# Down projection with weight panels of 512 rows by 512 columns in place of 1024 by 256, and one matmul bank a token tile held over two panels

## The chip, the cores and the metric

One core of one Trainium2 chip. The metric is the device time of one execution in microseconds (us). A core has TensorE (PE) for matmuls, whose weight loads are shown apart as PEld, VectorE (DVE), ScalarE (ACT), GpSimd (POOL) and SyncE (SP); SP and POOL issue most of the transfers.

## The reference

One inference step of a decoder layer of width 1024, over 2048 prompt tokens and 32 sample tokens (8 requests of 4). The part that the change touches is the MLP:

```python
D_MODEL = 1024; SEQ = 2048; DEC_BATCH = 8; DEC_SEQ = 4; D_FF = 4 * D_MODEL
...
    o = jnp.concatenate([y_a, y_b, y_c, y_d], axis=-1) @ w_out
    x = x + rms_norm(o, g_mix_post)
    f = rms_norm(x, g_ffn_pre)
    f = jnp.square(jax.nn.relu(f @ w_up)) @ w_down
    x = x + rms_norm(f, g_ffn_post)
```

Ahead of it stand an input projection (1024 to 2048 columns) and four parallel mixers (pooling, a 31-tap convolution, a chunked gating, a short convolution), whose outputs are concatenated for w_out. All arrays are float32.

## The kernel before

**Precision.** A projection in float32 is made of three matmuls in the format fp32r. Each operand is split in two parts: "hi" is its value rounded to fp32r, "lo" the rest. The helper `three` (L1772) issues hi x hi, hi x lo and lo x hi into the same bank, for each of K = 8 slices k of 128 rows of the contraction.

**Blocks and stages.** The tokens are worked in NB = 4 blocks of N1 = 512; the last block also carries the 32 sample tokens. First the input projection and the mixers run for all blocks ("I" panels), then block by block the output projection ("O"), and the MLP in Q = 4 quarters q of the hidden width: an up stage "U" makes 1024 hidden columns, and a down stage "D" multiplies them with 1024 rows of w_down and adds to the result of the earlier quarters in SBUF. In the last quarter of a block the O panels and the transposes of the next block stand among the D panels. The list `order` holds all panels.

**Panels.** A panel is a weight piece of 1024 rows by PC = 256 columns, [128, 8, 256] in SBUF. A stage has NP = 4 of them. Two slots s = j % 2 alternate. SP loads panel j into `raw[s]`; ACT rounds it into `w_hi[s]` (`split_hi`, L677), once the panel j - 2, which used the slot, is done on TensorE (`wait_panel`); DVE writes `w_lo[s]` (`split_lo`, L1127); TensorE starts panel j when `lo_ready` says so.

**Which operand moves.** In a U panel the weight slice is the stationary operand (128 x 128) and the tokens move: 512 columns of `act_hi` or `act_lo` at a time, 256 or 288 in the last block. The result has hidden columns on the partitions. ACT takes relu out of the bank and squares it (`squared_relu`, L949 and L951), DVE makes `u_hi[:, k]` and `u_lo[:, k]` (`u_parts`, L1498 and L1500); k runs with the panels, two a panel. In a D panel 128 tokens of `u_hi` or `u_lo` are stationary and the weight panel moves, 256 columns at a time. The result has tokens on the partitions; the four token tiles of a block lie two to a bank (`token_banks`), and the 32 sample tokens have a bank of their own.

**Banks.** Six banks `mm0` to `mm5` go round in a ring (`bank_of`). TensorE waits with `take_bank` until a bank is free; `bank_done` tells of its last matmul, `bank_free` that it was read. A D panel of quarter 0 is copied out by ACT (`d_copy`, L966), of quarters 1 to 3 added by DVE (`d_add`, L1516), to `f2_sb` (the profile's name for it is f_sb). On ACT and DVE a panel's split for j + 2 stands just ahead of the panel's last bank (`token_panel`).

Of the kernel before, what the change touches and what calls it, by code (L numbers as in the profile page):

```python
# [5 lines left out]
def hybrid_trunk_step(nc, x_prompt, x_sample, state_pool, state_conv, state_short, g_mix_pre, g_mix_post,  # L6
# [9 lines left out]
    PE, DVE, SC, GP = nc.tensor, nc.vector, nc.scalar, nc.gpsimd  # L16
# [53 lines left out]
    def token_banks(b):  # L70

        pairs = [[(2 * i + h, (2 * i + h) * P, P) for h in range(2)] for i in range(NCH // 2)]
        return pairs if b < NB - 1 else pairs + [[(NCH, N1, NS)]]

    NRING = 6
# [1 line left out]
    bank_of, wrote, freed, turn = {}, [0] * NRING, [0] * NRING, 0  # L79
    for j in range(J2, NPAN):  # L80
        kind, b, q, p = order[j]
        n_banks = 2 * len(halves(b)) if kind == "U" else len(token_banks(b))
        for i in range(n_banks):
            bank = turn % 4 if j < J2 + NP else (turn - 2 * NP + 4) % NRING
            turn += 1
            wrote[bank] += 1
            bank_of[j, i] = (bank, wrote[bank], freed[bank])
            freed[bank] += 1
        bank_of[j, "last"] = bank_of[j, n_banks - 1]
# [10 lines left out]
    with ctx:  # L100
# [261 lines left out]
        y_ready = sem("y_ready")  # L362
        y_out = sem("y_out")
        y_last = sem("y_last")

        OUT_SMALL = 2 + 3 * NB_S + 1 + 3
        WIN = [(0, 0, 2), (HEAD, 0, 4), (0, 1, 8), (HEAD, 1, 16)]
# [13 lines left out]
        def source(j):  # L381
            kind, b, q, p = order[j]
            if kind == "I":
                return w_in_v[:, :, COLS[p]:COLS[p] + PC]
            if kind == "O":
                return w_out_v[:, :, p * PC:(p + 1) * PC]
            if kind == "U":
                return w_up_v[:, :, q * D + p * PC:q * D + (p + 1) * PC]
            return w_dn_v[q][:, :, p * PC:(p + 1) * PC]

        def wait_panel(eng, j):

            if j < 0:
                return
            if j < NI:
                eng.wait_ge(zs_done, j + 1)
            elif j < J2:
                eng.wait_ge(tile_done, 2 * (j + 1))
            else:
                bank, done, _ = bank_of[j, "last"]  # L400
                eng.wait_ge(bank_done[bank], done)
# [59 lines left out]
        def _(sp):  # L461
# [16 lines left out]
            for j, (kind, b, q, p) in enumerate(order):  # L478
                s = j % 2
                if j not in part_no:  # L480
                    if j in (J2, J2 + 1):
                        sp.wait_ge(x_tr, 2 * NCH * NB)
                    elif s in raw_user:
                        sp.wait_ge(lo_ready, split_no[raw_user[s]])
                    if j >= 2:
                        sp.dma_start(raw[:, s, :, :], source(j)).then_inc(raw_full[s], 16)
                    raw_user[s] = j
                if j == 3:
                    sp.wait_ge(bias_ready, 1)
# [178 lines left out]
        def _(act):  # L668
# [284 lines left out]
            def d_copy(j, i):  # L953
                _, b, q, p = order[j]
                bank = bank_of[j, i][0]
                tiles = token_banks(b)[i]
                tile, n, nt = tiles[0][0], tiles[0][2], len(tiles)
                wait_bank(act, j, i)
                if b > 0:
                    act.wait_ge(y_out, 16 * NCH * b)  # L960
                elif p == 0:
                    act.wait_ge(sx_tr, 1)
                    act.wait_ge(out_small, 16 * OUT_SMALL)
                    if i == 1:
                        act.wait_ge(smp_st, 64)
                SC.activation(f2_sb[0:n, tile:tile + nt, p * PC:(p + 1) * PC],  # L966
                              mm[bank][0:n, 0:nt * PC].rearrange("p (h c) -> p h c", h=nt), ACT.Copy)\
                  .then_inc(bank_free[bank], 1)

            def y_squares(j, i):  # L970
                _, b, q, p = order[j]
# [21 lines left out]

            def token_panel(j, piece):
                _, b, q, p = order[j]
                n = len(token_banks(b))
                for i in range(n):
                    if i == n - 1:
                        split_hi(j + 2)
                    piece(j, i)  # L1000
# [118 lines left out]
        def _(dve):  # L1119
# [383 lines left out]
            def d_add(j, i):  # L1503
                _, b, q, p = order[j]
                bank = bank_of[j, i][0]
                tiles = token_banks(b)[i]
                tile, n, nt = tiles[0][0], tiles[0][2], len(tiles)
                f2 = f2_sb[0:n, tile:tile + nt, p * PC:(p + 1) * PC]
                if q == 1:
                    before = index("D", b, 0, p)  # L1510
                else:
                    before = index("D", b, q - 1, p)
                old, _, free = bank_of[before, i]
                dve.wait_ge(bank_free[old], free + 1)
                wait_bank(dve, j, i)
                DVE.tensor_tensor(f2, mm[bank][0:n, 0:nt * PC].rearrange("p (h c) -> p h c", h=nt), f2, ALU.add)\  # L1516
                   .then_inc(bank_free[bank], 1)

            def y_inverse(b, g=0):
# [31 lines left out]

            def token_panel(j, piece):
                _, b, q, p = order[j]
                n = len(token_banks(b))
                for i in range(n):
                    if i == n - 1:
                        split_lo(j + 2)
                    piece(j, i)
# [212 lines left out]
        def _(pe):  # L1771
# [272 lines left out]
            for j in range(J2, NPAN):  # L2044
# [16 lines left out]
                            i += 1  # L2061
                else:
                    hi, lo = (act_hi, act_lo) if kind == "O" else (u_hi, u_lo)
                    for i, bank_tiles in enumerate(token_banks(b)):
                        bank = take_bank(j, i)
                        for h, (tile, t0, n) in enumerate(bank_tiles):
                            for k in range(K):
                                if kind == "O" and p == 0 and k == 0:
                                    pe.wait_ge(mix_lo, no(b, tile) + 1)
                                if kind == "D" and p == 0 and i == 0 and h == 0:  # L2070
                                    pe.wait_ge(u_lo_ready, u_no(b, q, k, len(halves(b))))
                                last_mm = three(mm[bank][0:n, h * PC:(h + 1) * PC], hi[:, k, t0:t0 + n],
                                                lo[:, k, t0:t0 + n], w_hi[:, s, k, :], w_lo[:, s, k, :], k)
                            if h == len(bank_tiles) - 1:
                                last_mm.then_inc(bank_done[bank], 1)
                            if kind == "D" and q == Q - 1 and b < NB - 1:
# [58 lines left out]
```

## Time and profile before

| | |
|---|---|
| median of 3 runs | 2232.03 us (2230.04 to 2232.41) |
| the profiled execution's own time | 2230.47 us |
| its span | 2228.2 us |
| mean granted TensorE clock over the span | 0.983 |
| PE busy | 2122.0 us, 95% of the span |
| PEld busy (beside PE) | 1932.4 us, 87% |
| DVE, ACT, POOL busy | 1083.2, 754.6, 107.6 us |
| DMA traffic | 287.42 MB |

The profiled execution's own time is 2.27 us more than its span and 1.56 us less than the median of the runs. Sums below are made from durations of this one execution, and are set against its own time. A matmul's duration in the profile overlaps the next one's, since matmuls are pipelined; what one costs in a stream is the distance between two starts.

### The profile page before, as it was taken

To read this page: it belongs to the slowest core of one execution; us is meant where nothing else is said; L and a number is where in the kernel's file an instruction comes from. 1 tells how busy PE (TensorE), PEld (TensorE's weight loads), DVE (VectorE), ACT (ScalarE), POOL (GpSimd) and SP (SyncE) were. 2 spreads that over 40 slices of the span, in tenths; PEclk is the share of its full clock that TensorE was granted. 3 is DMA by queue.
4 is the path that set the end of the run, shared out by engine and by line. 5 is a ranking of instruction groups with operands and counts; after the bars stand their busy time and mean duration, and the time that the engine had idled before them with its cause. 6 is when DMAs were issued, how large, how long until landed. Compare 5 with 4: busy or idle time off the path is not lost.

```text
span 2228.2 us, 33002 instructions
## 1 busy us (share of the span) xinstructions
PE 2122.0 (95%) x14425; PEld 1932.4 (87%) x14425; DVE 1083.2 (49%) x1404; ACT 754.6 (34%) x1159; POOL 107.6 (5%) x190
## 2 busy tenths in 40 slices
PE   6999999994999999999999999999999989999997
PEld 5887778784798898989899898889899989999997
DVE  3687786866523334563333346533334553333334
ACT  4424232234233223443322344332324432314132
POOL 2011111110000000000000000000000000000000
PEclk9999999997899999999999999999999999999999
DMA  7754646553132223444233344533334333222231
GB/s 250 277 201 165 222 170 209 194 178 129 59 114 95 95 95 114 139 150 153 94 107 95 97 132 152 170 95 95 95 95 135 108 103 116 77 93 78 77 95 41
DMA packets 184836, 287.42 MB, mean 129 GB/s; under 512 B 5967, under 2 KB 162292, under 8 KB 176484
## 3 DMA queue, kind: packets, MB, share of 16 engines
q1 hardware_dynamic: 160868, 169.99, 23.9%
q0 software_dynamic: 22784, 114.28, 14.6%
q8 instruction: 114, 1.87, 0.3%
q10 hardware_dynamic: 1040, 1.05, 0.1%
q14 instruction: 30, 0.25, 0.0%
HBM read 245.01 MB, written 40.57 MB: 128 GB/s over the span
## 4 chain that ended last, share of the span: by engine, by line
PE 83%; DVE 7%; ACT 4%; DMA 3%; issue 2%; POOL 0%; ACTq 0%; POOLq 0%; DVEq 0%
PE mm L1773 27%; PE mm L1775 27%; PE mm L1774 27%; ACT w_hi L677 2%; DVE w_lo L1127 2%; DMA mixc<-mixT_scratch 1%; DVE conv L1171 1%; PE tr L1778 1%; DMA x_in<-in_x_prompt 1%; DMA raw<-in_w_in 1%; PE tr L2002 1%; ACT junk_y L976 0%; PE mm L1833 0%; PE tr L1799 0%; DVE f_sb L1516 0%
## 5 line engine op out<-in xcount | busy, mean ns | idle before, releaser
L1127 DVE TENSOR_TENSOR w_lo<-raw,w_hi 128x2048 fp32r<-128x2048 f32 x152 | 348.4, 2292 | 696.4 <-ACT w_hi L677 696.4
L1773 PE MATMUL mm<-act_hi,w_hi 128*128 128x512 f32 (+2 forms) x1728 | 632.2, 366 | 11.1 <-DVE act_lo L1484 5.8
L1775 PE MATMUL mm<-act_hi,w_lo 128*128 128x512 f32 (+2 forms) x1728 | 632.3, 366 | 0.0
L1774 PE MATMUL mm<-act_lo,w_hi 128*128 128x512 f32 (+2 forms) x1728 | 625.9, 362 | 0.0
L1773 PE MATMUL mm<-w_hi,u_hi 128*128 128x256 f32 (+1 forms) x2176 | 603.2, 277 | 1.7 <-DVE u_lo L1500 0.9
L1774 PE MATMUL mm<-w_lo,u_hi 128*128 128x256 f32 (+1 forms) x2176 | 600.8, 276 | 0.0
L1775 PE MATMUL mm<-w_hi,u_lo 128*128 128x256 f32 (+1 forms) x2176 | 600.8, 276 | 0.0
L677 ACT ACTIVATE w_hi<-raw 128x2048 fp32r<-128x2048 f32 x152 | 290.8, 1913 | 579.1 <-PE mm L1775 572.9
L1773 PEld LDWEIGHTS mm<-w_hi,u_hi 128*128 128x128 f32 (+1 forms) x2176 | 398.2, 183 | 4.9 <-DVE u_lo L1500 3.8
L1774 PEld LDWEIGHTS mm<-w_lo,u_hi 128*128 128x128 f32 (+1 forms) x2176 | 398.3, 183 | 1.1
L1775 PEld LDWEIGHTS mm<-w_hi,u_lo 128*128 128x128 f32 (+1 forms) x2176 | 398.2, 183 | 0.7
L1773 PEld LDWEIGHTS mm<-act_hi,w_hi 128*128 128x128 f32 x1728 | 328.3, 190 | 62.9 <-issue 14.9
L1774 PEld LDWEIGHTS mm<-act_lo,w_hi 128*128 128x128 f32 x1728 | 328.2, 190 | 57.1 <-issue 2.4
L1775 PEld LDWEIGHTS mm<-act_hi,w_lo 128*128 128x128 f32 x1728 | 327.5, 190 | 50.5
L1773 PE MATMUL mm<-w_hi,act_hi 128*128 128x256 f32 (+1 forms) x736 | 205.9, 280 | 7.0 <-DVE act_lo L1432 4.3
L1774 PE MATMUL mm<-w_lo,act_hi 128*128 128x256 f32 (+1 forms) x736 | 203.9, 277 | 0.0
L1775 PE MATMUL mm<-w_hi,act_lo 128*128 128x256 f32 (+1 forms) x736 | 203.9, 277 | 0.0
L949 ACT ACTIVATE square<-mm 128x512 f32<-128x512 f32 (+2 forms) x160 | 81.8, 511 | 257.7 <-PE mm L1775 255.1
L1171 DVE SCALAR_TENSOR_TENSOR conv<-g_ext,cst,conv 128x512 f32<-128x512 f32 x240 | 163.0, 744 | 0.7 <-ACT conv L800 0.7
L1498 DVE CAST u_hi<-square 128x512 fp32r<-128x512 f32 (+2 forms) x160 | 60.0, 375 | 187.6 <-ACT square L951 187.6
L1773 PEld LDWEIGHTS mm<-w_hi,act_hi 128*128 128x128 f32 (+1 forms) x736 | 131.2, 178 | 9.4 <-issue 5.1
L1774 PEld LDWEIGHTS mm<-w_lo,act_hi 128*128 128x128 f32 (+1 forms) x736 | 131.2, 178 | 2.0 <-issue 0.5
(244 smaller groups left out, 1341.7 us busy)
## 6 DMA issues: line engine op xcount, KB each, us to landing
raw<-in_w_ffn_up SPq DMA_DIRECT2D x64, 1024.0 KB, 5.4
raw<-in_w_ffn_down SPq DMA_DIRECT2D x64, 1024.0 KB, 5.2
w_hi<-whi_scratch POOLq DMA_DIRECT2D x24, 1024.0 KB, 5.2
w_lo<-wlo_scratch POOLq DMA_DIRECT2D x24, 1024.0 KB, 7.9
raw<-in_w_out SPq DMA_DIRECT2D x16, 1024.0 KB, 5.2
whi_scratch<-w_hi POOLq DMA_DIRECT2D x8, 1024.0 KB, 8.6
wlo_scratch<-w_lo POOLq DMA_DIRECT2D x8, 1024.0 KB, 10.8
mixc<-mixT_scratch POOLq DMA_DIRECT2D x16, 512.0 KB, 5.8
```

What stands on the lines that cost most here:

```text
L677: SC.activation(w_hi[:, s, :, :], raw[:, s, :, :], ACT.Copy).then_inc(hi_ready, 1)
L949: SC.activation(square[:, at % 2, 0:c1 - c0], mm[bank][:, 0:c1 - c0], ACT.Relu).then_inc(bank_free[bank], 1)
L1127: DVE.tensor_tensor(w_lo[:, s, :, :], raw[:, s, :, :], w_hi[:, s, :, :].bitcast(fp32), ALU.subtract)\
L1171: DVE.scalar_tensor_tensor(out=c, in0=g_ext[:, t, k:k + N1], scalar=col("conv_w", 2 * k + t), in1=c, op0=ALU.mult, op1=ALU.add).then_inc(c ...
L1498: DVE.tensor_copy(u_hi[:, k, c0:c1], square[:, at % 2, 0:c1 - c0]).then_inc(u_hi_ready, 1)
L1773: PE.matmul(out, whi, xhi, start=(k == 0), stop=False)
L1774: PE.matmul(out, whi, xlo, start=False, stop=False)
L1775: return PE.matmul(out, wlo, xhi, start=False, stop=(k == K - 1))
L1778: PE.matmul(bank[:, 0:n], headmean[:, :], src, start=True, stop=True).then_inc(done, 1)
L2002: last = PE.transpose(tr[hh][:, kk * P:kk * P + n], f_sb[0:n, m % 2, k * P:(k + 1) * P], ident[0:n, 0:n])
```

## The change

For the quarters q = 0, 1, 2 of each block (12 of the 16 down stages; `wide(j)` says which) the four panels of a stage keep their number and their size of 1 MB, but have another form. Panels 0 and 1 hold output columns 0 to 511, panels 2 and 3 columns 512 to 1023; the even one holds rows k = 0 to 3 of the contraction, the odd one k = 4 to 7. The slots are the same memory, seen as [128, 4, 512]. Each token tile takes a bank of its own (four, or five in the last block) in the even panel, and its accumulation is finished in the odd one. The moving operand is 512 weight columns. Since no bank is done in an even panel, a new semaphore `half_done` tells when its last matmul is through; ACT and DVE have only their split in an even panel, and read all banks out in the odd one.

```diff
+    def wide(j):
+        return order[j][0] == "D" and order[j][2] < Q - 1
+
+    def panel_banks(j):
+        banks = token_banks(order[j][1])
+        return [[t] for bank in banks for t in bank] if wide(j) else banks
...
-        n_banks = 2 * len(halves(b)) if kind == "U" else len(token_banks(b))
+        n_banks = 2 * len(halves(b)) if kind == "U" else len(panel_banks(j))
+        if wide(j) and p % 2:
+            for i in range(n_banks):
+                bank_of[j, i] = bank_of[j - 1, i]
+            bank_of[j, "last"] = bank_of[j, n_banks - 1]
+            continue
...
+            if wide(j):
+                return w_dn_v[q][:, p % 2 * (K // 2):(p % 2 + 1) * (K // 2), p // 2 * 2 * PC:(p // 2 + 1) * 2 * PC]
...
+            elif j in half_no:
+                eng.wait_ge(half_done, half_no[j])
...
             def d_copy(j, i):
...
-                elif p == 0:
+                elif p == 1:
...
-                SC.activation(f2_sb[0:n, tile:tile + nt, p * PC:(p + 1) * PC],
-                              mm[bank][0:n, 0:nt * PC].rearrange("p (h c) -> p h c", h=nt), ACT.Copy)\
-                  .then_inc(bank_free[bank], 1)
+                c = p // 2 * 2 * PC
+                SC.activation(f2_sb[0:n, tile, c:c + 2 * PC], mm[bank][0:n, :], ACT.Copy).then_inc(bank_free[bank], 1)
...
+                if j in half_no:
+                    split_lo(j + 2)
+                    return
...
+                    if wide(j):
+                        w_h, w_l = (as_panel(w[:, s, :, :], j) for w in (w_hi, w_lo))
+                        for i, ((tile, t0, n),) in enumerate(panel_banks(j)):
+                            bank = bank_of[j, i][0] if p % 2 else take_bank(j, i)
+                            for kk in range(K // 2):
+                                k = p % 2 * (K // 2) + kk
+                                if p < 2 and i == 0:
+                                    pe.wait_ge(u_lo_ready, u_no(b, q, k, len(halves(b))))
+                                last_mm = three(mm[bank][0:n, :], hi[:, k, t0:t0 + n], lo[:, k, t0:t0 + n],
+                                                w_h[:, kk, :], w_l[:, kk, :], k)
+                            if p % 2:
+                                last_mm.then_inc(bank_done[bank], 1)
+                        if p % 2 == 0:
+                            last_mm.then_inc(half_done, 1)
+                        continue
```

On TensorE the first tile of a down stage looks like this before; each group of three belongs to one slice k, and the eight that wait for `u_lo_ready` are k = 0 to 7 (block 0, quarter 1; shown are k = 0, the head of k = 1, and k = 7):

```order
L1773 MATMUL mm<-w_hi,u_hi 128x256 [waits u_lo_ready,bank_free4,lo_ready]
L1774 MATMUL mm<-w_lo,u_hi 128x256
L1775 MATMUL mm<-w_hi,u_lo 128x256
L1773 MATMUL mm<-w_hi,u_hi 128x256 [waits u_lo_ready]
...
L1773 MATMUL mm<-w_hi,u_hi 128x256 [waits u_lo_ready]
L1774 MATMUL mm<-w_lo,u_hi 128x256
L1775 MATMUL mm<-w_hi,u_lo 128x256
```

and like this in the changed kernel, where the lines of `three` are 1810 to 1812. The tile has four slices and goes over to the next bank:

```order
L1810 MATMUL mm<-w_hi,u_hi 128x512 [waits u_lo_ready,bank_free4,lo_ready]
L1811 MATMUL mm<-w_lo,u_hi 128x512
L1812 MATMUL mm<-w_hi,u_lo 128x512
L1810 MATMUL mm<-w_hi,u_hi 128x512 [waits u_lo_ready]
...
L1810 MATMUL mm<-w_hi,u_hi 128x512 [waits bank_free5]
L1811 MATMUL mm<-w_lo,u_hi 128x512
```

So the waits for k = 4 to 7 now stand at the head of panel 1, behind the four tiles of panel 0. A stage of 384 matmuls of 256 columns (480 in the last block, with the sample tile) becomes one of 192 (240) of 512 columns.

On ACT the four panels of block 0, quarter 0 read before (a copy takes a bank with two tiles of 256 columns, and the split stands between the two copies of a panel):

```order
L966 ACTIVATE f_sb<-mm 128x2x256 [waits out_small,sx_tr,bank_done0]
L677 ACTIVATE w_hi<-raw 128x2048 [waits bank_done1,raw_full0]
L966 ACTIVATE f_sb<-mm 128x2x256 [waits out_small,smp_st,sx_tr,bank_done1]
L966 ACTIVATE f_sb<-mm 128x2x256 [waits bank_done2]
L677 ACTIVATE w_hi<-raw 128x2048 [waits bank_done3,raw_full1]
L966 ACTIVATE f_sb<-mm 128x2x256 [waits bank_done3]
```

for panels 0 and 1, and in the changed kernel for the same two:

```order
L709 ACTIVATE w_hi<-raw 128x2048 [waits half_done,raw_full0]
L998 ACTIVATE f_sb<-mm 128x512 [waits out_small,sx_tr,bank_done0]
L998 ACTIVATE f_sb<-mm 128x512 [waits out_small,smp_st,sx_tr,bank_done1]
L998 ACTIVATE f_sb<-mm 128x512 [waits out_small,sx_tr,bank_done2]
L709 ACTIVATE w_hi<-raw 128x2048 [waits bank_done3,raw_full1]
L998 ACTIVATE f_sb<-mm 128x512 [waits out_small,sx_tr,bank_done3]
```

The number of copies and their size stay; none stands in the even panel, and three stand ahead of the split in the odd one.

## Rows read from the trace of the kernel before

**Rows 1.** The page: busy times and the chain that ended last

```profile
PE 2122.0 (95%) x14425; PEld 1932.4 (87%) x14425; DVE 1083.2 (49%) x1404; ACT 754.6 (34%) x1159; POOL 107.6 (5%) x190
...
PE 83%; DVE 7%; ACT 4%; DMA 3%; issue 2%; POOL 0%; ACTq 0%; POOLq 0%; DVEq 0%
PE mm L1773 27%; PE mm L1775 27%; PE mm L1774 27%; ACT w_hi L677 2%; DVE w_lo L1127 2%; DMA mixc<-mixT_scratch 1%; DVE conv L1171 1%; PE tr L1778 1%; DMA x_in<-in_x_prompt 1%; DMA raw<-in_w_in 1%; PE tr L2002 1%; ACT junk_y L976 0%; PE mm L1833 0%; PE tr L1799 0%; DVE f_sb L1516 0%
```

**Rows 2.** Windows, the twelve down stages: stretch, length, PE busy (matmuls), clock, DMA

```profile
613.64:657.30 43.66, 43.66 (x386) 1.00 0.40 122
701.46:745.44 43.98, 43.83 (x386) 1.00 0.30 96
...
1018.08:1062.04 43.96, 43.81 (x386) 1.00 0.43 132
...
1853.51:1907.94 54.43, 54.43 (x482) 1.00 0.27 88
...
sum 558.72, PE 557.52; mean PE 46.46
```

**Rows 3.** The same view, up stages of block 1, 512 token columns moving

```profile
1062.04:1106.19 44.15, 44.15 (x194) 1.00 0.30 96
```

**Rows 4.** Timeline of PE, block 3: up of 256 and 288 columns, then down

```profile
1847.54 0.28 PE L1773 MATMUL mm<-act_hi,w_hi 128*128 128x256 f32 x1
...
1850.34 0.29 PE L1773 MATMUL mm<-act_hi,w_hi 128*128 128x288 f32 x1
...
1853.51 0.28 PE L1773 MATMUL mm<-w_hi,u_hi 128*128 128x256 f32 x1
```

**Rows 5.** Timeline of PE in block 0 at a low clock, 512 columns moving

```profile
561.62 0.63 PE L1775 MATMUL mm<-act_hi,w_lo 128*128 128x512 f32 x1
562.05 0.63 PE L1773 MATMUL mm<-act_hi,w_hi 128*128 128x512 f32 x1
```

**Rows 6.** Windows, the stretch around rows 5: length, PE busy, clock, DMA

```profile
561.19:565.03 3.84, 3.84 (x10) 0.50 0.00 0
```

**Rows 7.** Timeline of PE, first tile of the down stage at 1018.08

```profile
1018.08 0.28 PE L1773 MATMUL mm<-w_hi,u_hi 128*128 128x256 f32 x1
...
1020.36 0.28 PE L1775 MATMUL mm<-w_hi,u_lo 128*128 128x256 f32 x1
1020.79 0.38 PE L1773 MATMUL mm<-w_hi,u_hi 128*128 128x256 f32 x1
1021.01 0.28 PE L1774 MATMUL mm<-w_lo,u_hi 128*128 128x256 f32 x1
```

**Rows 8.** Timeline of ACT, same stage

```profile
1018.28 0.60 ACT L949 ACTIVATE square<-mm 128x512 f32<-128x512 f32 x1 [4.25 <-PE mm L1775]
1018.91 0.63 ACT L951 ACTIVATE square<-square 128x512 f32<-128x512 f32 x1
...
1030.23 0.60 ACT L966 ACTIVATE f_sb<-mm 128x512 f32<-128x512 f32 x1 [8.88 <-DMA out<-f_sb]
1030.72 1.91 ACT L677 ACTIVATE w_hi<-raw 128x2048 fp32r<-128x2048 f32 x1
```

**Rows 9.** Timeline of DVE, same stage

```profile
1019.58 0.43 DVE L1498 CAST u_hi<-square 128x512 fp32r<-128x512 f32 x1 [3.44 <-ACT square L951]
1020.04 0.69 DVE L1500 TENSOR_TENSOR u_lo<-square,u_hi 128x512 fp32r<-128x512 f32 x1
...
1032.67 2.29 DVE L1127 TENSOR_TENSOR w_lo<-raw,w_hi 128x2048 fp32r<-128x2048 f32 x1 [6.54 <-ACT w_hi L677]
```

**Rows 10.** Lines with shapes apart: reads of the banks in down stages

```profile
L1516 DVE TENSOR_TENSOR f_sb<-mm,f_sb 128x512 f32<-128x512 f32 x96 | 65.9, 687 | 80.3 <-PE mm L1775 80.3
L966 ACT ACTIVATE f_sb<-mm 128x512 f32<-128x512 f32 x32 | 18.8, 591 | 75.4 <-PE mm L1775 48.7 <-DMA out<-f_sb 26.7
```

**Rows 11.** The page: transfers of weights, KB each, us to landing

```profile
raw<-in_w_ffn_up SPq DMA_DIRECT2D x64, 1024.0 KB, 5.4
raw<-in_w_ffn_down SPq DMA_DIRECT2D x64, 1024.0 KB, 5.2
```

More of the change, by code:

```diff
@@ L364, in hybrid_trunk_step @@
         y_last = sem("y_last")
+        half_done = sem("half_done")
         OUT_SMALL = 2 + 3 * NB_S + 1 + 3
@@ L388, in source, with as_panel @@
                 return w_up_v[:, :, q * D + p * PC:q * D + (p + 1) * PC]
+            if wide(j):
+                return w_dn_v[q][:, p % 2 * (K // 2):(p % 2 + 1) * (K // 2), p // 2 * 2 * PC:(p // 2 + 1) * 2 * PC]
             return w_dn_v[q][:, :, p * PC:(p + 1) * PC]
+        def as_panel(slot, j):
+            if wide(j):
+                return slot.rearrange("p k c -> p (k c)").rearrange("p (k c) -> p k c", k=K // 2)
+            return slot
+        half_no = {}
+        for j in range(NPAN):
+            if wide(j) and order[j][3] % 2 == 0:
+                half_no[j] = 1 + len(half_no)
         def wait_panel(eng, j):
@@ L485, in _ @@
                     if j >= 2:
-                        sp.dma_start(raw[:, s, :, :], source(j)).then_inc(raw_full[s], 16)
+                        sp.dma_start(as_panel(raw[:, s, :, :], j), source(j)).then_inc(raw_full[s], 16)
                     raw_user[s] = j
@@ L955, in d_copy @@
                 bank = bank_of[j, i][0]
-                tiles = token_banks(b)[i]
-                tile, n, nt = tiles[0][0], tiles[0][2], len(tiles)
+                tile, _, n = panel_banks(j)[i][0]
                 wait_bank(act, j, i)
@@ L995, in token_panel @@
                 _, b, q, p = order[j]
-                n = len(token_banks(b))
+                n = len(panel_banks(j))
+                if j in half_no:
+                    split_hi(j + 2)
+                    return
                 for i in range(n):
@@ L1505, in d_add @@
                 bank = bank_of[j, i][0]
-                tiles = token_banks(b)[i]
+                tiles = panel_banks(j)[i]
                 tile, n, nt = tiles[0][0], tiles[0][2], len(tiles)
-                f2 = f2_sb[0:n, tile:tile + nt, p * PC:(p + 1) * PC]
-                if q == 1:
-                    before = index("D", b, 0, p)
-                else:
-                    before = index("D", b, q - 1, p)
-                old, _, free = bank_of[before, i]
-                dve.wait_ge(bank_free[old], free + 1)
+                if wide(j):
+                    f2 = f2_sb[0:n, tile:tile + 1, p // 2 * 2 * PC:(p // 2 + 1) * 2 * PC]
+                else:
+                    f2 = f2_sb[0:n, tile:tile + nt, p * PC:(p + 1) * PC]
+                for t, _, _ in tiles:
+                    old, _, free = bank_of[index("D", b, q - 1, p // 2 * 2), t]
+                    dve.wait_ge(bank_free[old], free + 1)
                 wait_bank(dve, j, i)
-                DVE.tensor_tensor(f2, mm[bank][0:n, 0:nt * PC].rearrange("p (h c) -> p h c", h=nt), f2, ALU.add)\
+                DVE.tensor_tensor(f2, mm[bank][0:n, 0:2 * PC if wide(j) else nt * PC].rearrange("p (h c) -> p h c", h=nt), f2, ALU.add)\
                    .then_inc(bank_free[bank], 1)
@@ L1553, in token_panel @@
                 _, b, q, p = order[j]
-                n = len(token_banks(b))
+                n = len(panel_banks(j))
+                if j in half_no:
+                    split_lo(j + 2)
+                    return
                 for i in range(n):
@@ L2063, in _ @@
                     hi, lo = (act_hi, act_lo) if kind == "O" else (u_hi, u_lo)
+                    if wide(j):
+                        w_h, w_l = (as_panel(w[:, s, :, :], j) for w in (w_hi, w_lo))
[12 more added lines that the diff above has]
+                        continue
                     for i, bank_tiles in enumerate(token_banks(b)):
```

## Prediction

> **What bounds the kernel now.** I read the page first. PE is busy for 2122.0 of 2228.2 us, and the chain that ended last lies on it for 83%, 27% on each of the three lines of `three` [rows 1]. DVE and ACT are busy for half the time or less. So only two things can move the time: what a matmul costs in a full stream, and the few places where the stream stops.
>
> The windows over the twelve down stages that the change touches show both [rows 2]. Each stage of blocks 0 to 2 has 384 matmuls of 256 columns (the counts in the windows are one or two higher, since they take in the neighbours at the edges), each of block 3 has 480. They take 558.72 us together. The stages of block 3 take 54.43 us, or 113.4 ns a matmul. At that distance 384 take 43.55 us. The first stage takes 43.66; the other eight of blocks 0 to 2 take some 43.97 (two of them are shown), so about 0.42 us is lost in each of the eight.
>
> The timeline shows where. In the stage that begins at 1018.08, the first 20 matmuls come at 114 ns, then the one at 1020.36 is followed only at 1020.79, 0.43 us on, and that by one after 0.22 us [rows 7]; a usual pair would take 0.23 of these 0.65 us. The late matmul is number 22, the first of slice k = 7. It waits for `u_lo_ready`: relu at 1018.28, square at 1018.91, u_hi at 1019.58, and u_lo from 1020.04 to 1020.73 [rows 8, 9]. That chain begins when the last up matmul has ended, and the seven slices ahead of k = 7 cover only some 2.4 us of it.
>
> **The change part by part.**
>
> *The wait for the last hidden slices.* In the changed program the first tile of a stage uses only k = 0 to 3; k = 7 comes first in panel 1, behind 48 matmuls of 512 columns, some 10.9 us on. u_lo of k = 7 is ready 2.65 us into the stage [rows 7, 9], and that of k = 3 was made two up panels ago. The hole goes, in eight stages: 8 x 0.42 = 3.4 us less. Nothing else is late next: the weights of panel 0 were there already when the stream went in without a gap.
>
> *The distance of the matmuls.* 4896 of 256 columns (9 x 384 + 3 x 480) become 2448 of 512 columns. The trace has no matmul that streams 512 weight columns past a token tile. The rows bound it from both sides. From above: in the up stages 192 matmuls of 512 token columns take 44.15 us, 229.9 ns each, more than two of the 256 weight columns (226.8) [rows 2, 3]. From below: if what a matmul takes beyond one column per cycle is a fixed price for each. That price: at a granted clock of 1.2 GHz 512 columns take 0.43 us [rows 5, 6], which is one column a cycle; at 2.4 GHz 256 columns are then 106.7 ns, and the row says 113.4. If the 6.7 ns are paid once a matmul, 512 columns take 220.0 ns.
>
> I take 226.8, twice the old distance, because the rows of the up stages speak for a price by the column. In block 3 the same kind of matmul, token columns moving, comes with 256 and with 288 columns: 24 of 256 from 1847.54 to 1850.34 are 116.7 ns each, 24 of 288 from 1850.34 to 1853.51 are 132.1 [rows 4]; with 512 it is 229.9. From 256 to 512 columns the distance rises by 113.2 ns, not by 106.7, and from 256 to 288 by 15.4, not by 13.3. A fixed price would not rise at all. What is left over, 3.3 ns a matmul, separates the two forms at equal length (116.7 against 113.4), and hangs on which operand moves, or where it lies in memory, rather than on how many columns there are. The moving operand here is the weight tile, as before. So the sum for this part is nil, with -16.6 us at one end (2448 x 6.8) and +7.6 us at the other (2448 x 3.1).
>
> The Trainium skill ("TensorE: Matmul & The Clock Gate", section "Back-to-back issue gap") gives the gap of two warm matmuls as the columns over 2.4 GHz plus some 2.5 ns. That is a fixed price; by it each merged pair would save 2.5 ns, 6.1 us in all. The trace does not agree with its figures: it has 113.4 where the rule gives 109.2, and 229.9 where it gives 215.8 [rows 2, 3].
>
> *Weights.* A panel stays 1 MB, and 48 matmuls of twice the length take as long as 96. The source rows are 2 KB in place of 1 KB. A load lands in 5.2 us [rows 11], and it has more than a panel of 10.9 us for it, so a change in its speed is hidden. The split of the next panel but one takes 1.91 us on ACT and 2.29 us on DVE; in the stage shown it ends at 1034.96 [rows 8, 9], and panel 2 begins at some 1040.3 (1018.08 + 0.42 + 192 x 0.1134), so 5.3 us are left. There the split had even stood behind a copy that waited 8.88 us for an output transfer [rows 8]; in the even panels of the changed kernel no copy stands ahead of it. In the odd ones three reads do, 0.59 us on ACT and 0.69 us on DVE [rows 10], and each of their banks is full 2.7 us before the next, so they are done when the split can begin. Price: nil; without that cover a late split would stop TensorE for its whole delay.
>
> *Banks and reads.* A bank is now held for over a panel. A stage takes four of the six in each pair of panels (five in block 3), in turn. The next pair begins with the free one or two, and its second or third tile, 2.7 us or more on, takes a bank that was full three quarters of a panel earlier. The last bank of a pair is read behind a split, 4.3 us + 0.69 us after its last matmul, and is taken again two or more tiles into a later panel. Price: nil, cover 2.7 us or more. The reads keep their number and width.
>
> **Sum.** The profiled execution took 2230.47 us. Less 3.4 us it is 2227.1 us. The median of the runs is 1.56 us above that execution, so 2228.6 us, 0.15% less than before. A difference under 0.2% (4.5 us) is about what a measurement of this kernel cannot tell from no change.
>
> **The rivals.**
>
> *A fixed price for each matmul* (faster). The new distance is 220.0 ns: 2448 x 0.220 = 538.6 us in place of 558.7, so -20.1 us and 2211.9 us. For it: the trace has no row of this form, and one column a cycle holds at the low clock. Against it: the 113.2 ns that 256 more token columns cost. A third of the price would be 3.4 + 5.5 us less, 2223.1 us. Chance 0.10 for the full price, 0.05 for about a third of it. The rule of "TensorE: Matmul & The Clock Gate" in the Trainium skill is this rival with 2.5 ns as the price: 3.4 + 6.1 us less, 2222.5 us.
>
> *The up stages' distance* (slower). If the 3.1 ns that 512 token columns have over twice 113.4 come from the long stream itself, the down stages take 2448 x 0.2299 = 562.8 us, 4.1 us more than now though the holes are gone: 2236.1 us. It decides from 228.2 ns on, where the loss eats the 3.4 us. For it: it is the only row with 512 columns in this format at full clock. Against it: 256 token columns carry the same surplus. Chance 0.15; about half of that would measure over +0.2%.
>
> *The hole only moves.* If the first tile still stopped, at its head or at panel 1, for 0.42 us, nothing would change: 2232.0 us. It would need k = 3 or the weights of panel 0 to be late, and both were there. Chance 0.06.
>
> *The forecast* has the rest, 0.64: holes gone, twice the distance. Its own range is 2225 to 2231 us, and with the scatter of the runs (1 to 2 us) about a sixth of it falls beyond -0.2%.
>
> **How the numbers follow.** Faster by over 0.2%: 0.15 + 0.11 = 0.26. Slower by over 0.2%: 0.08. Within: 0.66. The range from 2221 to 2238 us takes in the forecast, the moved hole, the up stages' distance and a third of the fixed price, and leaves out the full fixed price and mishaps, not over 0.2.
>
> **What would show it.** In the profile after, the distance of two matmuls of 512 columns in a down stage: 226.8 (forecast), 220 (fixed price) or 230 (up stages' distance). A wide stage of blocks 0 to 2 should last 43.5 us, of block 3 54.4 us, with no gap at k = 7 in its first tile and none at the head of panel 1. The up stages should stay at 44.15 us, and the fourth quarters should keep their hole, which the change does not reach. The forecast is wrong if TensorE waits for ACT or DVE at a panel's head (a bank or a split late), or if the time moves outside the twelve stages.

## The result and the profile after

The changed kernel takes 2247.18 us (median of 4 runs, 2244.35 to 2247.47) against 2231.03 us (4 runs, the three from before and one more, 2229.93 to 2232.41): ratio 1.0069, interval 1.0052 to 1.0087, that is 12 to 19 us slower. The forecast was 2228.6 us, range 2221 to 2238. The profiled execution took 2247.47 us with a span of 2245.6 us (before 2230.47 and 2228.2).

The page of the changed kernel, against [rows 1, 11]: busy times, chain, and the loads of the down weights.

```profile
PE 2137.6 (95%) x11977; PEld 1831.2 (82%) x11977; DVE 1082.5 (48%) x1400; ACT 755.4 (34%) x1157; POOL 107.2 (5%) x190
...
PE 84%; DVE 7%; ACT 4%; DMA 3%; issue 2%; POOL 0%; ACTq 0%; POOLq 0%; DVEq 0%
...
raw<-in_w_ffn_down SPq DMA_DIRECT2D x64, 1024.0 KB, 5.0
```

There are 2448 matmuls fewer, and PE is busy 15.6 us longer. The windows over the same stages, against [rows 2] (stretch, length, PE busy with the matmuls, granted clock, DMA share, GB/s):

```profile
617.62:662.29 44.67, 44.67 (x195) 1.00 0.40 119
706.45:751.03 44.58, 44.58 (x193) 1.00 0.31 95
...
1026.07:1070.65 44.58, 44.58 (x193) 1.00 0.42 130
...
1867.14:1922.85 55.71, 55.71 (x242) 1.00 0.27 85
...
sum 568.44, PE 568.44; mean PE 47.37
```

Two things are read here. Length and busy time are equal in every stage, where before 43.96 stood beside 43.81: TensorE no longer stops. And still each stage is longer: 44.58 us over 192 matmuls is 232.2 ns each, 55.71 over 240 is 232.1. Together they take 568.44 us in place of 558.72, +9.7 us. It is the same at a DMA share of 0.31 and of 0.42, so it isn't the transfers. An up stage of block 1, against [rows 3], hasn't moved:

```profile
1070.65:1114.82 44.17, 44.17 (x194) 1.00 0.28 96
```

The timeline of PE shows the head of the down stage at 1026.07 and, 48 matmuls on, the head of its panel 1, the places of [rows 7]:

```profile
1025.84 0.39 PE L1812 MATMUL mm<-act_hi,w_lo 128*128 128x512 f32 x1
1026.07 0.39 PE L1810 MATMUL mm<-w_hi,u_hi 128*128 128x512 f32 x1
1026.30 0.39 PE L1811 MATMUL mm<-w_lo,u_hi 128*128 128x512 f32 x1
...
1036.97 0.40 PE L1812 MATMUL mm<-w_hi,u_lo 128*128 128x512 f32 x1
1037.21 0.39 PE L1810 MATMUL mm<-w_hi,u_hi 128*128 128x512 f32 x1
1037.44 0.40 PE L1811 MATMUL mm<-w_lo,u_hi 128*128 128x512 f32 x1
```

No gap stands at either: the hole is gone, and nothing took its place.

**Where the 17.4 us of the two spans lie.** The first down stage begins at 617.62 us in place of 613.64, +4.0 us, in a part that the change doesn't touch. The twelve stages are +9.7. From the first down stage to the end there are 1628.0 us in place of 1614.6, so 3.7 us lie between and behind the stages. Windows over the part ahead of the first down stage, of the kernel before and of the changed one:

```profile
0.00:613.64 613.64, 540.98 (x2898) 0.96 0.54 186
```

```profile
0.00:617.62 617.62, 545.63 (x2897) 0.95 0.54 185
```

PE's busy time rises by 4.65 us for the same matmuls, at a slightly lower granted clock. The experiments below bear on whether this comes with the change.

### The profile page after: what moved, and what is told of

Its sections match the earlier page's. It is cut to its first block, busy times and chain, and to the rows that moved or that the text cites. A ratio compares the mean times of both kernels' runs of the same rounds, so it can differ in the third digit from the quotient of the medians.

```text
span 2245.6 us, 28084 instructions
## 1 busy us (share of the span) xinstructions
PE 2137.6 (95%) x11977; PEld 1831.2 (82%) x11977; DVE 1082.5 (48%) x1400; ACT 755.4 (34%) x1157; POOL 107.2 (5%) x190
## 4 chain that ended last, share of the span: by engine, by line
PE 84%; DVE 7%; ACT 4%; DMA 3%; issue 2%; POOL 0%; ACTq 0%; POOLq 0%; DVEq 0%
PE mm L1812 27%; PE mm L1810 27%; PE mm L1811 27%; DVE w_lo L1160 2%; ACT w_hi L709 2%; DMA mixc<-mixT_scratch 1%; DVE conv L1204 1%; PE tr L1815 1%; DMA x_in<-in_x_prompt 1%; DMA raw<-in_w_in 1%; PE tr L2039 1%; ACT junk_y L1006 0%; PE tr L1836 0%; PE mm L1870 0%; DVE f_sb L1550 0%
## 5 line engine op out<-in xcount | busy, mean ns | idle before, releaser
L1810 PE MATMUL mm<-w_hi,u_hi 128*128 128x512 f32 (+3 forms) x1360 | 474.5, 349 | 0.4
L1812 PE MATMUL mm<-w_hi,u_lo 128*128 128x512 f32 (+3 forms) x1360 | 473.2, 348 | 0.0
L1811 PE MATMUL mm<-w_lo,u_hi 128*128 128x512 f32 (+3 forms) x1360 | 471.7, 347 | 0.0
L1811 PEld LDWEIGHTS mm<-w_lo,u_hi 128*128 128x128 f32 (+1 forms) x1360 | 249.6, 184 | 40.8
L1812 PEld LDWEIGHTS mm<-w_hi,u_lo 128*128 128x128 f32 (+1 forms) x1360 | 249.6, 184 | 40.6
L1810 PEld LDWEIGHTS mm<-w_hi,u_hi 128*128 128x128 f32 (+1 forms) x1360 | 249.8, 184 | 39.7 <-DVE u_lo L1533 1.0
```

What stands on the lines that cost most here:

```text
L1810: PE.matmul(out, whi, xhi, start=(k == 0), stop=False)
L1811: PE.matmul(out, whi, xlo, start=False, stop=False)
L1812: return PE.matmul(out, wlo, xhi, start=False, stop=(k == K - 1))
```

## The experiments

Each time is given against runs of the kernel before that were made beside it. The expectations weigh, by these names or in words, two main readings of the 232.2 ns; other names are explained where they stand. LOCK: a stream of 256 columns falls into a steady rhythm without surplus, other streams don't, and whether it does hangs on where the tiles lie. LENGTH: a matmul of 512 weight columns costs more by itself, wherever the tiles lie.

**The wide panels with matmuls of 256.** Panels, banks, waits and reads of the changed kernel; only the first and last matmul of a bank stay whole.

```diff
+            def pieces(b, q):
+                return slice(0, PC), slice(PC, 2 * PC)
...
+                                for m, (st, w) in enumerate(((hi, w_h), (hi, w_l), (lo, w_h))):
+                                    whole = (k, m) in ((0, 0), (K - 1, 2))
+                                    for c in (slice(0, 2 * PC),) if whole else pieces(b, q):
+                                        last_mm = PE.matmul(mm[bank][0:n, c], st[:, k, t0:t0 + n], w[:, kk, c],
```

> The changed kernel with its panels, banks and waits, but each matmul of 512 weight columns issued as two of 256 (the first and the last of a bank stay whole, 16 of 192 in a stage). In the changed kernel a wide stage of blocks 0 to 2 takes 44.58 us, 232.2 ns a matmul of 512 columns. Theory LENGTH (the long stream itself costs more than two short ones): the halves come at 113.3 to 113.5 ns, a stage takes 43.6 to 43.7 us, and the time falls to about 2228 us, 3 us under the kernel before, since the hole at k = 7 stays closed. Rival PANEL (what costs is the new form of the panels: rows of 2 KB, a bank kept open over two panels): the halves come at 116 ns or more, a stage stays at 44.5 us and the time near 2245 us.

Measured: 2238.07 us (11 runs) against 2232.98, ratio 1.0020 [1.0011, 1.0029]. Two thirds of the loss go; the time and the stages lie between what LENGTH and PANEL had asked for, and neither came out as it stands. Windows: one wide stage, then in a stage the whole matmul, the 11 of 256 behind it, and the next 11 (the counts in brackets take in neighbours).

```profile
706.08:750.23 44.15, 44.15 (x370) 1.00 0.31 96
```

```profile
1114.63:1114.86 0.23, 0.23 (x4) 1.00 0.00 0
1114.86:1116.15 1.29, 1.29 (x13) 1.00 0.00 0
1116.15:1117.39 1.24, 1.24 (x13) 1.00 0.00 0
```

Behind a matmul of 512 columns the first 11 of 256 cost 117 ns each, the next 11 come at 113. That they come to 113 ns in the new panels speaks against PANEL. So the 113.4 ns of [rows 2] are not the price of a column alone; they are a rhythm that a run of equal 256-column matmuls reaches after about ten here, and that one matmul of another width breaks. That, with the surplus of the 16 whole ones, is also why these stages take 44.15 us and not 43.55.

How long it takes to settle differs. In the kernel before, the 256-column matmuls of the stage at 1018.08 come straight behind 512-column ones of the up stage:

```profile
1018.21 0.28 PE L1774 MATMUL mm<-w_lo,u_hi 128*128 128x256 f32 x1
...
1018.43 0.28 PE L1773 MATMUL mm<-w_hi,u_hi 128*128 128x256 f32 x1
```

The next 17 up to 1020.36 [rows 7] take 113.5 ns each, so it had settled after three; and the hole at k = 7 doesn't break it, the 14 from 1021.01 to 1022.60 take 113.6 ns.

**A ruler of widths.** As in the last kernel, but each stage has a width of its own, as two pieces that overlap in the middle (the overlap is added twice, so the output is not the reference's, and the execution is longer by the added columns, 2438.23 us).

```diff
+WIDTHS = {(0, 0): 256, (0, 1): 272, (0, 2): 288, (1, 0): 320, (1, 1): 352, (1, 2): 384,
+          (2, 0): 416, (2, 1): 448, (2, 2): 480, (3, 0): 512, (3, 1): 496, (3, 2): 264}
+return (slice(0, wd), slice(2 * PC - wd, 2 * PC))[0:1 + (wd < 2 * PC)]
```

> A ruler, not a candidate: in each of the twelve wide stages a 512-column matmul is replaced by two overlapping ones of a width of its own (256, 264, 272, 288, 320, 352, 384, 416, 448, 480, 496, and 512 once), so that columns in the overlap are added twice and the output is not the reference's. Read is the distance of two matmuls by width. If the price beyond one column a cycle were fixed for each matmul, the distance would be columns / 2.4 + 6.7 ns plus a surplus. If it goes by the column: columns x 0.4427 ns plus a surplus. LENGTH: 113.3 at 256, and a surplus over 0.4427 ns a column that appears somewhere above 256 and is 5 to 6 ns at 512; where it begins (at once at 264, or gradually to 512) is open. Rival PLACE (the surplus comes from where the moving row starts and ends in memory): it jumps from width to width without order, since the second piece starts at another address each time.

The windows of its stages, in the order of the list:

```profile
614.36:658.62 44.26, 44.26 (x370) 1.00 0.39 120
702.79:750.48 47.69, 47.69 (x369) 1.00 0.29 89
794.64:844.79 50.15, 50.15 (x370) 1.00 0.26 85
1029.14:1084.34 55.20, 55.20 (x370) 1.00 0.33 105
...
1232.72:1297.76 65.04, 65.04 (x369) 1.00 0.21 65
...
1596.49:1670.99 74.50, 74.50 (x370) 1.00 0.17 57
...
2007.61:2063.32 55.71, 55.71 (x242) 1.00 0.26 85
...
2262.44:2320.55 58.11, 58.11 (x463) 1.00 0.24 74
```

A stage of blocks 0 to 2 has 16 whole matmuls (3.71 us) and 352 pieces, one of block 3 has 20 (4.64 us) and 440. That gives 121.5 ns for 264 columns, 124.9 for 272, 131.9 for 288, 146.3 for 320, 174.2 for 384, 201.1 for 448 and 232.1 for 512. The settled 113.33 ns over 256 columns are 0.4427 ns a column; above that price stand 4.6, 4.5, 4.4, 4.6, 4.2, 2.8 and 5.5 ns a matmul, and at the four widths not named 2.7 to 5.6. So there is a price by the column and one of 3 to 6 ns by the matmul, at every width but the settled 256: it is there at once at 264 columns and does not grow with the length. From 288 to 480 columns both pieces of a pair lie as the given ones do modulo 128 bytes; at 264, 272 and 496 the second one lies elsewhere, without standing out. Why the surplus is lower at 416 and 448 columns is not shown. The same surplus stands in the up stages of [rows 3]: 229.9 - 226.7 = 3.2 ns.

**The tiles moved by 32 or 320 bytes.** SBUF tiles lie behind each other in the order of their declarations. From their sizes, counted from the first tile, w_hi and w_lo begin at a multiple of 128 bytes and act and u 64 beyond one, and all their slices keep that place. A small tile declared ahead of `raw` moves the weights and leaves act and u. In the changed kernel this is `eps` (32 bytes), and in another kernel `cst` (320 bytes):

```diff
+        eps = sb("eps", [P, 1])
         raw = sb("raw", [P, 2, K, PC])
...
+        cst = sb("cst", [P, NROW])
         raw = sb("raw", [P, 2, K, PC])
```

> The changed kernel with the weight tiles raw, w_hi and w_lo 32 bytes further on in memory (they started at a multiple of 64 bytes, now at 32 beyond one). PLACE: the distance of the 256-column matmuls of the fourth quarters rises from 113.3 ns (to 116 or so, as in the up stages of block 3), and that of the 512-column ones changes by some ns as well. LENGTH: neither moves by over 0.3 ns (113.3 and 232.2).

> The same with 320 bytes in place of 32: still a multiple of 64, another place within 256 and 1024 bytes. PLACE: if blocks of 256 bytes or more count, the 512-column distance moves away from 232.2 ns; if only 64 bytes count, it stays while the kernel with 32 bytes moved. LENGTH: 113.3 and 232.2 ns as before.

2277.72 and 2256.53 us (one execution each) against 2232.98. Then the 32 bytes in the kernel before and, timed, in the changed one:

> The kernel before, with raw, w_hi and w_lo 32 bytes further on, nothing else changed. In the changed kernel this shift took the 256-column matmuls of the fourth quarters from 113.6 to 118.3 ns and the 512-column ones only from 232.2 to 233.4. Theory LOCK (a steady stream of 256-column matmuls settles, after some ten of them, into a rhythm without surplus, at 113.3 ns, and only where the operands lie right; streams of other widths never do, and pay 3 to 8 ns a matmul whatever the width): all 256-column weight streams go to 118 ns, a wide stage of blocks 0 to 2 to 45.4 us or a little more, and the time to 2282 to 2290 us. Rival LENGTH (a long stream costs more than two short ones as such): the shift does nothing to the 256-column streams of this kernel, 43.98 us a stage, and the time stays below the shifted changed kernel.

> The changed kernel with the same 32 bytes, timed beside the one before with them. LOCK: 2277 us, and so faster than the shifted kernel before by 8 to 12 us (12 stages at 44.8 us in place of some 45.5, and no hole): the sign of the change turns with the place of the weight tiles. LENGTH: it stays the slower one of the two, by some 15 us, as without the shift.

The kernel before rises to 2282.67 us (ratio 1.0219 [1.0205, 1.0233] to 2232.35) by 32 bytes alone. The changed one takes 2277.59 (1.0199 [1.0185, 1.0213]): here it is the faster form. Windows, the kernel before with 32 bytes: two down stages, an up stage, and 144 output matmuls of 256.

```profile
714.38:760.14 45.76, 45.71 (x386) 1.00 0.30 93
...
1896.46:1953.11 56.65, 56.65 (x482) 1.00 0.26 84
...
1085.04:1130.05 45.01, 45.01 (x194) 1.00 0.29 94
```

```profile
1341.43:1358.47 17.04, 17.04 (x146) 1.00 0.40 125
```

And the changed kernel with 32, then with 320 bytes, a down and an up stage each:

```profile
714.34:759.14 44.80, 44.80 (x194) 1.00 0.30 94
...
1086.04:1131.04 45.00, 45.00 (x193) 1.00 0.29 94
```

```profile
793.58:838.08 44.50, 44.50 (x194) 1.00 0.31 95
...
1071.47:1116.04 44.57, 44.57 (x193) 1.00 0.30 95
```

The 256-column matmul goes from 113.4 to 118.0 ns (56.65 us / 480), the 512-column one only from 232.2 to 233.3. The twelve stages take 581.6 us in the old form and 571.1 in the new: the sign turns with the placement, which rules LENGTH out. Of these 10.5 us the times of the whole kernels show 5.1.

**act moved instead of the weights.** The kernel before, `x_stats` declared behind act_lo, so that act begins 64 bytes lower, at a multiple of 128.

```diff
+        act_hi = sb("act_hi", [P, K, NX], f32r)
+        act_lo = sb("act_lo", [P, K, NX], f32r)
         x_stats = sb("x_stats", [P, 3, NCH])
...
-        act_hi = sb("act_hi", [P, K, NX], f32r)
-        act_lo = sb("act_lo", [P, K, NX], f32r)
```

> The kernel before with x_stats moved behind act_lo, which puts act_hi and act_lo 64 bytes lower, at multiples of 128 bytes, as the weight tiles are. LOCK with the place of the moving operand alone deciding: the up stages lose their surplus (512 columns at 226.7 in place of 230.0, stages of 43.5 in place of 44.15 us; 256 columns in block 3 at 113.3 in place of 116.7), 11 x 0.63 + some 4 us in block 3 + some in the input panels, 2218 us or less. If the place of the stationary operand counts as well, the output panels change too (113.5 ns now), in either direction. If 512 columns never settle, the up stages stay between 229 and 233 ns, whatever the place.

2244.88 us, 1.0053 [1.0038, 1.0069] to 2232.35. Windows of a down stage, an up stage, and 144 output matmuls:

```profile
1868.71:1923.17 54.46, 54.46 (x483) 1.00 0.27 88
...
1071.49:1116.07 44.58, 44.58 (x194) 1.00 0.30 95
```

```profile
1322.60:1339.72 17.12, 17.12 (x147) 1.00 0.39 123
```

The same 144 output matmuls in the kernel before, and in the changed one with 320 bytes:

```profile
1311.76:1328.08 16.32, 16.32 (x146) 1.00 0.40 130
```

```profile
1323.79:1340.91 17.12, 17.12 (x146) 1.00 0.38 124
```

The reading that only the moving operand's place counts fell here. In the output stages act is the stationary operand, the weights that move lie where they lay, and their matmuls go from 113.3 to 118.9 ns (17.12 us / 144). The up stages get worse, though act now begins at a "rounder" place. Both numbers are those of the 320-byte run (17.12 us, and 44.57 for its up stages), where the weights had moved and act hadn't: what the two runs share is the distance between the operands, modulo 128.

**u alone moved, in both forms.**

```diff
+        pad = sb("pad", [P, 8], to=p2)
         u_hi = sb("u_hi", [P, K, NX], f32r, to=p2)
```

> The kernel before, with 32 bytes of padding ahead of u_hi. Only u_hi, u_lo and two scratch tiles behind them move; raw, w_hi, w_lo and act stay. u is the stationary operand of the down stages, so those alone can change; up and output stages are the control. RELATIVE PLACE (what a matmul costs depends on how the stationary and the moving operand lie to each other, modulo some small power of two): the 256-column matmuls of the down stages lose the steady 113.4 ns and come at 118 to 119 ns as when the weights were moved by 32 bytes, so wide stages (the same panels as in the kernel before) last 45.4 to 45.8 us in blocks 0 to 2 in place of 43.97, the sixteen down stages together cost 25 to 30 us more, and the time is 2257 to 2263 us; up stages stay at 44.16. MOVING OPERAND ALONE (only the place of the weights counts, in the down stages, and the stationary one only elsewhere): nothing changes, 2232 us.

> The changed kernel with the same 32 bytes ahead of u_hi. RELATIVE PLACE: 512-column matmuls never had the steady rhythm, so a wide stage moves little, by at most the 0.2 us seen when the weights moved (44.58 to 44.8 us); the four stages of the fourth quarters, still of 256 columns, lose some 1.6 to 2 us each. Time 2253 to 2258 us, that is below e9_u_shift32 by 3 to 6 us: the new form is then the faster one, with the up stages untouched this time. MOVING OPERAND ALONE: nothing changes, 2247 us.

The old form takes 2249.13 us, ratio 1.0081 [1.0064, 1.0098], the new one 2245.08, 1.0061 [1.0046, 1.0076], to 2231.42. A down stage of block 0, one of block 3 and an up stage of block 1, old form, then a down stage of the new one:

```profile
795.65:840.82 45.17, 45.09 (x386) 1.00 0.30 94
...
1970.86:2026.93 56.07, 56.07 (x483) 1.00 0.24 76
...
1070.84:1114.99 44.15, 44.15 (x194) 1.00 0.29 96
```

```profile
792.14:836.52 44.38, 44.38 (x194) 1.00 0.31 95
```

Moving the stationary operand alone costs the twelve down stages of the old form 16 us (574.46 us against 558.72), and the up stages nothing. The direction was as expected; the old form's loss per stage was smaller (45.17 us, not 45.4 to 45.8), and both times lie some 8 us below the ranges expected. The new form even gains 0.2 us a stage. In ns a matmul, by the place of the token tile (u or act) less that of the weight tile, modulo 128 bytes:

| | 64 (as given) | 32 | 0 | 96 |
|---|---|---|---|---|
| 256 columns, down or output | 113.4 | 118.0 | 118.9 | 116.8 |
| 512 columns, down | 232.2 | 233.3 | 231.8 | 231.1 |
| 512 columns, up (tokens move) | 229.9 | 234.4 | 232.1 | not run |
| 256 columns, up in block 3 (tokens move, 24 in a row) | 116.7 | 118.3 | 117.8 | not run |

The values at 64, 32 and 96 in the first row are those of a stage of block 3, where one matmul in five has only 32 tokens; the one at 0 is of output matmuls. Only 256 weight columns at 64 bytes are free of surplus: 256 token columns at the same distance take 116.7 ns. In each of the other three columns two old matmuls cost more than one new one (236.0 against 233.3, 237.8 against 231.8, 233.6 against 231.1).

That the distance counts modulo 128 bytes is a statement on averages of a stage. The slices k of act and u lie 2176 bytes apart, which is 128 beyond a multiple of 512, so a stage always runs through all places that differ by 128 within 512. The single matmuls show it: in the output stage of the 320-byte run their starts are 117, 118, 117, 122, 120, 127, 118, 125, 117, 113, 120 and 113 ns apart, and the same again, within a nanosecond or so, for each next twelve, that is four slices. What one unsettled matmul costs thus hangs on more than the place modulo 128.

**Part of the stages in the new form.** Block 3 alone, and blocks 0 to 2 alone (reads and waits follow the form of each stage):

```diff
-        return order[j][0] == "D" and order[j][2] < Q - 1
+        return order[j][:2] == ("D", NB - 1) and order[j][2] < Q - 1
```

> The new form in the three stages of block 3 alone; the nine of blocks 0 to 2 stay as in the kernel before. The twelve stages cost 3 x (55.71 - 54.43) = 3.8 us more. STAGES ONLY (what the changed kernel loses beside its stages, 4.0 us ahead of the first down stage and 4.7 us in the output and last down stages, is scatter of waits and clock between executions): the time is 3.8 us above before, 2235 to 2237 us, and what lies beside the twelve stages differs from before by less than 3 us. ELSEWHERE (that loss comes with the new form, in the stages around it): it is small here too as there is only one output stage behind no wide stage; the loss stays under 1 us in blocks 0 to 2.

> The complement: the new form in the nine stages of blocks 0 to 2, the old one in block 3. The stages cost 9 x 0.6 = 5.9 us more. STAGES ONLY: 5.9 us above before, 2237 to 2239 us, and together with the run of block 3 the sum of both differences is 9 to 10 us, less than the 16 us of the whole change. ELSEWHERE: 12 to 14 us above before, 2243 to 2246 us, with the output stages of blocks 0 to 2 half a microsecond or more longer each and PE waiting in them for w_lo.

2236.16 us (11 runs), ratio 1.0019 [1.0010, 1.0028], and 2239.52 us (5 runs), 1.0033 [1.0021, 1.0046], to 2230.95. A stage of each form, of the first and of the second kernel:

```profile
704.78:748.75 43.97, 43.82 (x385) 1.00 0.31 97
...
2062.70:2118.41 55.71, 55.71 (x243) 1.00 0.24 76
```

```profile
702.65:747.23 44.58, 44.58 (x194) 1.00 0.31 95
...
2066.14:2120.56 54.42, 54.42 (x482) 1.00 0.26 78
```

Each stage pays its price alone, 1.28 and 0.61 us. By the ratios the kernels lose 2 to 6 and 5 to 10 us, where the stages give 3.8 and 5.9; ELSEWHERE had asked for 12 to 14 in the second, which fell. In the first the part ahead of the first down stage took 616.96 us (span 2234.2), in the second 613.82 (span 2236.4), with the same program there. The twelve wide stages of the ruler of widths stand behind 614.36 us, and the old form with only u moved, which this part doesn't use, behind 617.27. The +4.0 us of that part are thus scatter between executions or programs, not the change.

**The hole closed without wide matmuls.** The kernel before; in panel 0 of the down stages of blocks 0 to 2 both banks are taken at once, in the order tile 0 k = 0 to 3, tile 2 k = 0 to 3, tile 0 k = 4 to 7, tile 2 k = 4 to 7, then tiles 1 and 3.

```diff
+banks = [take_bank(j, i) for i in range(2)]
+for h in range(2):
+    for k0 in (0, 4) if h == 0 else (0,):
+        for i, bank_tiles in enumerate(token_banks(b)):
+            tile, t0, n = bank_tiles[h]
+            for k in range(k0, k0 + 4 if h == 0 else K):
...
```

> The kernel before with one change for the hole at k = 7 alone: in panel 0 of every down stage of blocks 0 to 2 TensorE takes both banks at once and goes tile 0 k 0 to 3, tile 2 k 0 to 3, tile 0 k 4 to 7, tile 2 k 4 to 7, then tiles 1 and 3, all 256 columns wide. If the hole is worth what the rows gave (0.42 us in each of 11 stages, fourth quarters among them) and closing it costs nothing: stages of 43.6 us, 4.6 us less, about 2227.5 us beside 2232. If the hole only moves (the first copy or the split late): 2232 us.

```profile
788.68:832.21 43.53, 43.53 (x386) 1.00 0.31 97
...
1849.54:1903.97 54.43, 54.43 (x483) 1.00 0.27 88
```

2228.69 us (11 runs) against 2232.35, ratio 0.9980 [0.9971, 0.9989]: faster than both kernels. A stage is 0.44 us shorter, which is the whole hole, at the old distance; the twelve take 555.20 us in place of 558.72.

## Why the prediction was wrong

*"The wait for the last hidden slices"* was right: the hole is gone in the eight stages, nothing is late instead, and the run that closed it alone has 3.5 us less in its twelve stages, beside the 3.4 forecast (3.7 us less in all, 2 to 6 by the interval, counting the fourth quarters too).

*"The distance of the matmuls"* failed. It took 226.8 ns, nil for the sum; the stages show 232.2, which is 2448 x 5.4 = 13.2 us. With the holes' 3.4 us taken off that makes the +9.7 us seen (13.2 - 3.4 = 9.8). The step rightly argued for a price by the column, 0.443 ns. It went wrong with the 3.3 ns that remained between the up and the down form, which it kept out of the new form: "hangs on which operand moves, or where it lies in memory", and with "the moving operand here is the weight tile, as before" it carried the surplus-free distance over to 512 columns. In fact the surplus is the ordinary case, and the 256-column stream of the down stages was the exception, by its width, by the operand that moves and by the place of both. The step had named two of these and not the width. The upper bound, 229.9, failed too: it was taken from a row in which the tokens move, and at the same distance of 64 bytes the new form, in which the weights move, lies 2.3 ns above it. The rival "The up stages' distance" had the sign right, with a chance of 0.15, but not the mechanism: it gave the surplus to "the long stream itself", which the moved tiles ruled out, and its 2236.1 us lie 11 us below the 2247.18 measured. What was set against it, "256 token columns carry the same surplus", is true, and should have been read as a sign that the surplus is the rule and the settled stream the exception.

The rule of the Trainium skill ("TensorE: Matmul & The Clock Gate", section "Back-to-back issue gap"), the columns over 2.4 GHz plus some 2.5 ns for each matmul, came near in form. Unsettled matmuls do pay a fixed part and merging them saves it: at 32 bytes two old ones cost 236.0 and one new one 233.3. Settled ones don't pay it, so there is nothing to save. Its figures don't fit: it gives 109.2 ns for 256 columns and 215.8 for 512, where the stages show 113.4 and 232.2.

*"Weights"* and *"Banks and reads"*, nil, were right: the loads land in 5.0 us, and length equals busy time in all twelve stages. *"The hole only moves"* fell, and so did "A fixed price for each matmul": a matmul of 512 columns cost more than two of 256 at this placement, and 231.1 to 233.3 ns at the others, nowhere near 220.0.

*Outside the stages* the prediction had no term. The 4.0 us ahead of them are scatter, as told. The 3.7 us between and behind them are 1.8 in the output stage of block 1 and the down panels behind it, 2.0 in those of block 2, 1.1 in the output stage of block 3, and 1.1 less in block 3's first up stage. The first two are within what one kernel shows: the changed kernel with 32 bytes, profiled twice, has 44.84 and 41.78 us for the same panels behind block 1's output stage. In block 3's output stage ACT waits for the transfer of mixc longer, and TensorE for the weights split behind it (its longest stop lasts 2.17 us from one start to the next, before 1.03). The rows of ACT in the kernel before, in the changed one, in the one with the new form in blocks 0 to 2 alone, and in the one with it in block 3 alone:

```profile
1701.47 1.06 ACT L900 ACTIVATE act_hi<-mixc 128x1024 fp32r<-128x1024 f32 x1 [7.57 <-DMA mixc<-mixT_scratch]
```

```profile
1716.19 1.06 ACT L932 ACTIVATE act_hi<-mixc 128x1024 fp32r<-128x1024 f32 x1 [8.62 <-DMA mixc<-mixT_scratch]
```

```profile
1709.05 1.06 ACT L932 ACTIVATE act_hi<-mixc 128x1024 fp32r<-128x1024 f32 x1 [8.59 <-DMA mixc<-mixT_scratch]
```

```profile
1704.28 1.06 ACT L932 ACTIVATE act_hi<-mixc 128x1024 fp32r<-128x1024 f32 x1 [7.62 <-DMA mixc<-mixT_scratch]
```

This stage takes 55.5 to 55.9 us in the three kernels of the given placement whose blocks 0 to 2 have the old panels, and 56.6 to 59.1 in the four with the new ones. So the wide panels seem to delay it by 1 to 3.6 us; with one profiled execution each this is not shown, nor is the way it would come about. The times point the same way: at all three placements where both forms were timed, the new one loses 4.6 to 6.4 us more than its twelve stages account for (16.2 us against 9.7; with 32 bytes it gains 5.1 of 10.5, with u moved 4.1 of 8.7). How much of that is this stage and how much scatter stays open.

## What to carry over

Before merging matmuls to save on their number, measure what one costs in its stream against a price by the column: if it is already at that price, there is nothing to save, and the longer one may fall out of the rhythm that made it so. A surplus that stands in every other row is the rule, and the row without it is what needs a reason. Move a tile by 32 bytes before you believe that a form of matmul is cheap or dear; the placement was worth more here (2.2%) than the change (0.7%). A hole at the head of a stage can be closed by the order of the matmuls alone.

## What was not expected of the hardware

Thirty-two bytes in the place of the weight tiles cost 50 us of 2232, with no instruction changed; what counts for a stage is the distance between the stationary and the moving operand modulo 128 bytes, as far as steps of 32 bytes tell (four places were tried, with these tiles). Within a stage the single unsettled matmul varies by up to 15 ns, in a pattern that comes again every four slices of 2176 bytes. A stream of 256 weight columns settles at 113.3 ns, starting from 117 to 121: after about ten matmuls behind a whole one in the kernel with halves, after three behind the up stage at 1018.08. Why only this width settles, only with weights moving and only at 64 bytes, is not shown: no view of the profile shows how TensorE reads its operands.
